# A two-block transformer kernel: the step-size stage opens the first state-space group, and the second norm comes from sums formed in the output stage

## What is computed

```python
def rms(x):      return x * rsqrt(mean(x * x, -1) + 1e-6)
# first block, end
x1 = x + merged @ w_out[layer]
h  = rms(x1) * g_final                     # input of the second block
# second block, mixer
u  = rms(h) * m_norm
zxbcdt = u @ m_in                          # z, conv channels (x, B, C), and dt: 32 columns, one per head
xbc = silu(causal_depthwise_conv(xbc, conv_w, conv_b))
dt  = softplus(dt + dt_bias)
A   = -exp(A_log)
# per chunk of 128 tokens
acum = cumsum(dt * A)                      # decays of the scan come from exp(acum)
...                                        # chunked scan over x, B, C with dt and acum
h = h + gated_and_normed(y) @ m_out
```

## Time and profile before

| | |
|---|---|
| median of 3 runs | 3327.12 us (3324.29 to 3329.75) |
| profiled execution | 3331.93 us, of it the span from first to last instruction 3330.4 us |
| busy: PE, DVE, ACT, POOL | 3112.3 us (93%), 1831.2 (55%), 1394.0 (42%), 682.2 (20%) |
| mean granted TensorE clock, share of full speed | 0.967 |
| output stage, PE's products | 1295.8 to 1385.9 us |
| step-size stage, up to PE's first product of the state-space stage | 1385.9 to 1460.2 us |
| state-space stage | 1460.2 us to about 2270 us |

### The profile page before, as it was taken

How to read it: one execution, slowest core, us unless ns; L and a number is a source line. 1 busy time by engine, 2 the same in 40 slices (tenths; PEclk the granted TensorE clock), 3 DMA queues, 4 the chain that set the end, 5 groups by cost and what they waited for, 6 DMA issues and landing times. The chain is left out here.

```text
span 3330.4 us, 41838 instructions
## 1 busy us (share of the span) xinstructions
PE 3112.3 (93%) x15516; PEld 2601.6 (78%) x15516; DVE 1831.2 (55%) x2485; ACT 1394.0 (42%) x2093; POOL 682.2 (20%) x455
## 2 busy tenths in 40 slices
PE   6999999999999999779999999998899999997799
PEld 5788887888888887657787877776778888886677
DVE  4344222666666533356757666576357777776343
ACT  4333212555555422234334242343246666666331
POOL 3100002222222200211001020010234444443110
PEclk9999999999999999879999999998999999998899
DMA  2111222121111223102111121211111111111321
GB/s 98 41 50 42 70 76 64 58 64 58 51 58 57 93 103 139 33 27 74 48 58 64 45 83 39 70 51 57 69 53 41 43 39 39 39 39 45 120 71 55
DMA packets 55763, 201.69 MB, mean 61 GB/s; under 512 B 6432, under 2 KB 9376, under 8 KB 55328
## 3 DMA queue, kind: packets, MB, share of 16 engines
q1 hardware_dynamic: 46176, 166.76, 15.2%
q0 software_dynamic: 9408, 32.51, 3.1%
HBM read 167.66 MB, written 23.20 MB: 57 GB/s over the span
## 5 line engine op out<-in xcount | busy, mean ns | idle before, releaser
L114 ACT ACTIVATE whi<-wraw 128x1024 fp32r<-128x1024 f32 x208 | 218.4, 1051 | 452.4 <-PE out_D L127 67.6
L119 DVE TENSOR_TENSOR wlo<-wraw,whi 128x1024 fp32r<-128x1024 f32 x173 | 232.8, 1345 | 154.7 <-ACT whi L114 151.1
L125 PE MATMUL ssm_D<-x1hi,whi 128*128 128x512 f32 x640 | 260.2, 407 | 4.4 <-DVEq L1792 4.4
L125 PE MATMUL b_D<-x1hi,whi 128*128 128x512 f32 x640 | 256.0, 400 | 8.5 <-DVEq L1002 6.6
L127 PE MATMUL ssm_D<-x1hi,wlo 128*128 128x512 f32 x640 | 253.3, 396 | 0.0
L126 PE MATMUL ssm_D<-x1lo,whi 128*128 128x512 f32 x640 | 252.8, 395 | 0.0
L126 PE MATMUL b_D<-x1lo,whi 128*128 128x512 f32 x640 | 251.2, 392 | 0.0
L127 PE MATMUL b_D<-x1hi,wlo 128*128 128x512 f32 x640 | 251.0, 392 | 0.0
L2232 DVE TENSOR_TENSOR_SCAN stick_keep<-stick_keep 128x896 f32<-128x896 f32 (+7 forms) x128 | 215.7, 1686 | 43.4 <-ACT stick_keep L2140 42.1
L2371 POOL TENSOR_TENSOR stick_rows<-stick_rows,stick_keep 128x896 f32<-128x896 f32 (+7 forms) x128 | 162.5, 1272 | 272.6 <-DVE stick_keep L2232 272.3
L125 PE MATMUL stick_D<-x1hi,whi 128*128 128x512 f32 x512 | 210.6, 411 | 8.1 <-DVE x1lo L152 8.1
(11 more groups left out here) (413 smaller groups left out, 7982.1 us busy)
## 6 DMA issues: line engine op xcount, KB each, us to landing
wraw<-w_dram SPq DMA_DIRECT2D x208, 512.0 KB, 3.6
sq<-acum_rows SPq DMA_DIRECT2D x32, 512.0 KB, 3.7
att_bias<-alibi_dram SPq DMA_DIRECT2D x16, 512.0 KB, 3.6
stack<-stack POOLq DMA_DIRECT2D x32, 256.0 KB, 3.7
x_sb<-xT_dram SPq DMA_DIRECT2D x8, 512.0 KB, 8.6
branch_a<-sq POOLq DMA_DIRECT2D x8, 512.0 KB, 3.5
y_b<-att_y POOLq DMA_DIRECT2D x8, 512.0 KB, 3.0
f<-y_b SPq DMA_DIRECT2D x2, 2048.0 KB, 8.7
```

Source lines behind the costliest of these rows:

```text
L114: act.activation(self.whi[:, s, :, :], self.wraw[:, s, :, :], ACT.Copy).then_inc(self.w_hi, 1)
L119: dve.tensor_tensor(self.wlo[:, s, :, :], self.wraw[:, s, :, :], self.whi[:, s, :, :].bitcast(F32), ALU.subtract).then_inc(self.w_lo, 1)
L125: pe.matmul(out, self.whi[:, s, w0, :], xhi[:, k, cols], start=start, stop=False)
```

## The change

The output stage gets its own function, `stage_out`, written out without a loop. x is no longer brought into a tensor of its own: SP loads tile k of x into `f_sb` as soon as DVE has split that tile of `merged` (8 transfers of 512 KB, ahead of the stage's weight loads on SP). For tiles 0 to 6 ACT squares x1 and also x1 * g_final, and POOL keeps two sums, in `acc` and in `R`. The stage also loads and splits `w_dt`, now 32 columns wide, and multiplies the gains g_final * m_norm into `decay.gain`. h is not formed here.

`stage_dt` is gone. In `stage_ssm`, which is written out four times instead of looping on all engines, group 0 begins with what is left of it:

- `start()` on ACT and DVE: split x1 * decay.gain into `xhi`/`xlo` (unnormed), square tile 7 twice; POOL adds those squares. Since the norm factors are one number a token, they are put in later: R of the first group's scaling now holds the product of both norms' factors, 1/root1 * 1/root2, with root2 worked out from the second sum and 1/root1.
- On PE: `decay_tile` (the 48 products for dt), the first half of tile 0, `base_sums` (both norm sums), `turn_rows`, the second half, then `spread_factor(rt)`; after tile 1 `spread_factor(K.rtok)`, after tile 2 `decay_sums`; after tile 5 a wait for all of `f_done`, `copied` and `v_step`.
- On DVE behind tile 0 `step_sizes` (the softplus), behind tile 2 `decay_sums`, behind tile 3 `decay_ends`, and behind tiles 2, 3, 4 and 5 two tiles each of `final_norm`, which forms h = x1 * g_final * (1/root1) in `f_sb` from the factor spread in `pY`, and counts `f_done`.
- On ACT behind tile 2 `copy_sums`, behind tile 3 `decay_factors` (three exponentials). SP writes the sums to DRAM between two weight loads of the group.

```diff
@@ stage_out @@
+def stage_out(K, f_sb, xhi, xlo, x_dram, decay):
...
+                for k in range(KT):
+                    sp.wait_ge(x_lo, k + 1)
+                    sp.dma_start(f_sb[:, k, :], x_dram[:, k, :]).then_inc(x_land[k], 16)
+                K.load_ahead(sp, name)
...
+                    for i in range(2):
+                        if n >= 2:
+                            act.wait_ge(acc_done, 2 * n + i - 3)
+                        act.activation(K.sq[:, i, :] if n else accs[i][:, :], f_sb[:, n, :], ACT.Square,
+                                       scale=K.gain("g_final", n) if i else 1.0).then_inc(sq_done, 1)
...
@@ stage_ssm, pe @@
-                    for c in range(6):
+                    if g == 0:
+                        decay_tile()
+                        units(g, 0, 0, KT)
+                        base_sums()
+                        turn_rows()
+                        units(g, 0, KT, 2 * KT)
+                        pe.wait_ge(rt_step, 5)
+                        spread_factor(rt)
+                        units(g, 1, 0, 16)
+                        pe.wait_ge(r_base, 1)
+                        spread_factor(K.rtok)
+                        units(g, 2, 0, 16)
+                        decay_sums()
+                    for c in range(3 if g == 0 else 0, 6):
                         units(g, c, 0, 16)
+                    if g == 0:
+                        pe.wait_ge(copied, 3)
+                        pe.wait_ge(v_step, 13)
+                        pe.wait_ge(f_done, KT)
...
-                with pe.Fori(0, GROUPS) as g:
+                for g in range(GROUPS):
                     group(g)
@@ stage_ssm, act @@
+                def decay_factors():
+                    act.wait_ge(v_step, 12)
+                    act.activation(e_acum[:, :], acum[:, :], ACT.Exp).then_inc(a_step, 1)
+                    act.activation(dte[:, :], dte[:, :], ACT.Exp).then_inc(a_step, 1)
+                    act.activation(e_end[:, :], end[:, :], ACT.Exp).then_inc(a_step, 1)
...
                         act.activation(dst, dst, ACT.Silu).then_inc(cv_s, 1)
+                        if g == 0 and c == 2:
+                            copy_sums()
+                        if g == 0 and c == 3:
+                            decay_factors()
@@ stage_ssm, dve @@
+                def decay_ends():
+                    dve.wait_ge(a_step, 6)
+                    step(dve.tensor_tensor(dte[:, :], dte[:, :], dt[:, :], ALU.mult))
+                    step(dve.tensor_scalar(acum[:, :], acum[:, :], -1.0, None, ALU.mult))
+
+                def final_norm(k0, k1):
+                    dve.wait_ge(spread_base, 2)
+                    for k in range(k0, k1):
+                        dve.scalar_tensor_tensor(f_sb[:, k, :], f_sb[:, k, :], K.gain("g_final", k), pY[:, :],
+                                                 ALU.mult, ALU.mult).then_inc(f_done, 1)
...
                         split(g, c + 2)
+                        if g == 0:
+                            if c == 0:
+                                step_sizes()
+                            elif c == 2:
+                                decay_sums()
+                            elif c == 3:
+                                decay_ends()
+                            if c >= 2:
+                                final_norm(2 * c - 4, 2 * c - 2)
```

More of the change, by code:

```diff
@@ L1262, in _ @@
             @block.tensor
             def _(pe):
[L1264 to L1286, removed]
@@ L1287, in _ @@
-                last.then_inc(t_step, 1)
-                pe.matmul(pA[:, 0:W], tri[:, :], dA[:, :], start=True, stop=True)
-                pe.matmul(pA[:, W:2 * W], K.ones[:, :], dA[:, :], start=True, stop=True).then_inc(t_step, 1)
+                for n in range(KT):
+                    pe.wait_ge(K.w_lo, n + (n0 + 1))
+                    if n >= 2:
+                        pe.wait_ge(added, n - 1)
+                    K.dense(pe, D[:, n % 2, :], n % 2, xhi, xlo, x_lo if n == 0 else None).then_inc(mm, 1)
@@ L1311, in _ @@
[L1311 to L1317 removed]
+                act.activation(decay.hi[:, :, :], raw[:, :, :], ACT.Copy).then_inc(w_done, 1)
@@ new lines, in _ @@
+                dve.wait_ge(w_done, 1)
+                dve.tensor_tensor(decay.lo[:, :, :], raw[:, :, :], decay.hi[:, :, :].bitcast(F32), ALU.subtract)
+                dve.tensor_tensor(decay.gain[:, :], K.vec[:, VEC["g_final"]:VEC["g_final"] + KT],
+                                  K.vec[:, VEC["m_norm"]:VEC["m_norm"] + KT], ALU.mult)
+                for n in range(KT):
+                    dve.wait_ge(mm, n + 1)
+                    dve.wait_ge(x_land[n], 16)
+                    dve.tensor_tensor(f_sb[:, n, :], D[:, n % 2, :], f_sb[:, n, :], ALU.add).then_inc(added, 1)
+                    K.split_lo(dve, n // 2 + (n0 // 2 + 1), n % 2)
@@ L1395, in stage_ssm @@
         xd_odd = scratch[:, GT - 1, :]
+        W = NC * SH
+        with ExitStack() as shared:
+            small = lambda n, shape: shared.enter_context(nc.sbuf_tensor("dt_" + n, shape, F32))
+            rows = small("rows", [SH, S])
+            v, e, l, d, r, dA, end = (small(n, [P, W]) for n in ("v", "e", "l", "d", "r", "dA", "end"))
+            part2, root2, rtok2, rt = (small(n, [P, NC]) for n in ("part2", "root2", "rtok2", "rt"))
         with ExitStack() as shared:
@@ L1640, in _ @@
                 act.sem_inc(cb_copy, 1)
-                with act.Fori(0, GROUPS) as g:
+                start()
+                for g in range(GROUPS):
                     group(g)
@@ L1794, in _ @@
                     dve.sem_inc(q, 1)
-                with dve.Fori(0, GROUPS) as g:
+                start()
+                for g in range(GROUPS):
                     group(g)
```

276 lines of the change are left out of this document (166 added, 110 removed).

## The result

The kernel after takes 3301.27 us (median of 4 runs, 3292.86 to 3305.29), the kernel before on the same chip 3328.43: a ratio of 0.9915, with a 95% interval of 0.990 to 0.993. The profiled execution after took 3305.29 us, its span 3303.8, against 3331.93 and 3330.4 before: 26.6 us less by either. The forecast was 3300.5 for the median and 3305.3 for the profiled run.

The account below looks back on a forecast made before the run. PE bounds the state-space stage; a chain through ACT, DVE and POOL bounds the hole before it. Terms sum to 117.3 us against 142.5; with 1.4 for one wait, gain 26.6: 3327.1 - 26.6 = 3300.5 us, range 3286 to 3314.

Parts of the forecast that it names:

- The hole: Stretch from the output stage's last product to the state-space stage's first, 73.8 us before, bound by an ACT, DVE, POOL chain.
- Item 2: From the last output product to the decay tile's first product PE idles 6.9 us.
- Item 3: Decay tile of 48 products, 14 of them slow: 13.8 us, with DVE's splits staying ahead of PE.
- rival B: Clock stays low at the start, through decay tile, sums and tile 0: gain about 5 us, 3322 us; chance 0.10.
- Item 5: Small products between the convolution tiles (base sums, turn, two spreads, cumulative sums): together 9.3 us.
- Items 6 to 8: PE's waits for DVE ahead of tiles 1, 2 and 5: 2.2, 0.8 and 2.9 us.
- Item 9: PE's wait ahead of the z products until all of h is written: 10.3 us, then 2.9 us for a slow restart.
- +2.9 for the restart and -1.4 for one wait: Z products restart slowly, 2.9 us more; PE's wait for DVE's weighing in the first z tile goes, 1.4 us less.
- A: Written-out loops shorten PE's waits for DVE in all four groups: 15 us more gain, 3286 us; chance 0.14.
- C: The waits keep the clock down through tile 5: 64 us lost, 3362 us; chance 0.06.
- The fail sign: The prediction fails if one of the three later groups changes by more than 3 us.
- Item 10's limit: Slow products follow a wait of 1.98 us but not 1.76; waits ahead of tiles 1 and 5 cost 1.8 each, net 2.8.

Follow-up runs that it names:

- `sums_apart`: The kernel after with the two sets of norm sums parted, the first right behind the decay tile, the second eight units later: 3300.28 us in one run.
- `ends_later`: The kernel after with DVE's two tiles of h in tile 3 ahead of the two steps that need ACT's exponentials: 3295.74 us in one run.
- `r_halves`: The kernel after with DVE's copy of R in two halves, each ahead of the scaling that needs it: 3298.85 us in one run.
- `late_wait`: The kernel after with PE's three waits moved from ahead of the first z product to behind the first 14 z units: 3287.96 us, ratio 0.9882.
- `loops_only`: The kernel before with only the state-space stage's group loops written out on all five engines: 3317.36 us against 3326.12, ratio 0.9971.
- `placed`: The kernel after with moved waits, parted sums, h first and R in halves, plus three small tensors laid where y_sb will be: 3274.36 us, ratio 0.9843.
- `loops_again`: A second look at the kernel before with only the state-space stage's group loops written out: 3318.04 us in one run.
- `apart`: The kernel after with the small products in one piece ahead of the six convolution tiles, no longer between them: 3308.78 us, ratio 0.9939.
- `split_later`: The kernel after with moved waits, parted sums, h first, R in halves, and DVE's first output weight split moved behind the skip: 3283.81 us, ratio 0.9873.

## Why the prediction was right, point by point

**The hole** was sized well: 115.7 us up to the first z product where the sum without the slow restart had 114.4.
- Item 2, first product: 6.5 us, forecast 6.9. Item 3, decay tile: 13.3 against 13.8; DVE's splits stayed ahead, so rival B did not happen.
- Item 5, small products: 4.8 for base sums and turn against 4.5, 2.65 for the cumulative sums against 2.7. Wrong was that nothing follows from them: 12 products behind the base sums were slow and cost 2.4 us. The text had it only as a bound ("a third slow stretch, 1.8 more"). `sums_apart` and the three kernels built on it show that the norm sums in one piece are its cause.
- Items 6 to 8: waits of 2.2, none and 2.6 us, forecast 2.2, 0.8 swallowed, and 2.9 (item 8's own terms add up to 14.0 behind the tile's end, not the 13.8 it states, which would make 3.1). All three stand on DVE's time to spare in a tile, and `ends_later` and `r_halves` show that reading right.
- Item 9: 9.8 us against 10.3, and products slow from 1502.4 to about 1507. `late_wait` puts its worth, with the restart, at 11.8.
- The Trainium skill ("ScalarE: Activation LUTs", What ACT_TABLE_LOAD costs) charges 1.38 us of drain with each table load. The load here began 0.01 us after the Silu's end and took 1.28 us, and the exponential began 0.02 us after that (1473.46 and 1474.76), so the trace does not agree, and the wait ahead of tile 5 came out by the row.

**The rest of the stage** came out right for wrong reasons. The sum gave it +2.9 for the restart and -1.4 for one wait; measured is nothing, 744.9 us from the first z product to the next stage in both. In it are at least four things: the restart; the weighing's waits, 3.5 us less, not because PE stands first (the step named in the sum) but because the loops are written out, as `loops_only` shows without any stand; one slow stretch less, in the fourth group; and 3.6 us more for output products that follow each other more slowly (47.1 to 47.2 us a group instead of the 46.2 of `placed`), which nobody looks for in a diff. The last two were not in the text at all. That the four cancel, and the whole came out at the forecast, is luck.

**The rivals.** A was half right: written-out loops alone bring 8.8 us to the kernel before, and halve the weighing's waits, though not the skip's. The argument against it, that register rows are worked off while the engine is busy, failed: DVE's three taps take 3.92 us in a row now and took 4.14 in loops. The Trainium skill ("Runtime: NRT & Kernel Launch", Instruction fetch mechanics) names a stall at the branch as one price of a loop; the trace shows none on PE, which is busy 10.00 of 10.00 us at the turn both in loops and in `loops_only` (1660 to 1670 us), and shows the price in the waits for DVE. In the kernel after little of it is seen: the new layout takes back 3.6 us, and slow products stand behind three of the four skip's waits. C did not happen; after each of the waits the clock was back within 9 to 12 products.

**The fail sign** that the prediction set, a change of more than 3 us in one of the later groups, did not come: their pitch is 201.1 us on average in both. But this mean hides a gain and a loss.

## What to carry to other kernels

See how much of a gain comes from the shorter chain before working on what hides it: with the small products in one piece, this change kept 21.5 of the 25.0 us between the marks. Where several semaphores are waited for at one place, see which of the next instructions need each; moving one wait behind 14 units of products was worth 11.8 us. After a change of allocation compare the spacing of products in stages that the diff does not touch.

## What the runs showed of the hardware

**The clock falls behind small products too.** Behind 4.8 us of norm sums and turn without a wait the granted clock was 0.5 for the next products; cut to 2.4 us, with 24 large products ahead, it stayed full. Ahead of the convolution tiles a wait of 1.67 us was not followed by slow products, waits of 2.2 and more always were; in the scan 1.97 to 2.00 us ahead of the last turn went both ways, and of the waits for the weighing 1.63, 1.86 and 2.01 were followed by slow products, those of 1.61 and less were not. Item 10's limit between 1.76 and 1.98 was too simple. The Trainium skill ("TensorE: Matmul & The Clock Gate", What's actually happening) says that the gate judges on a schedule of its own which runs on regardless of the program. That would fit one wait with two outcomes; no run here shows the schedule itself, and why `loops_only` and `loops_again` had none in eight groups stays open.

**Where a tensor lies can set the pace of products**: 226.8 to 227.0 ns against 232.4 to 233.2 at the full clock, with the stage's tensors, y among them, 896 bytes further up. Other things that lie there were moved too, so that it is y's own place is likely, not shown.

**DVE and POOL took turns.** While POOL's last two adds of squares ran, DVE's last split took 3.44 us instead of 1.28, and POOL's second add 3.38 instead of 2.40:

```profile
1400.11 2.46 POOL L1935 TENSOR_TENSOR acc<-acc,sq 128x1024 f32<-128x1024 f32 x1 [17.09 <-ACT sq L1584]
1402.53 3.38 POOL L1935 TENSOR_TENSOR R<-R,sq 128x1024 f32<-128x1024 f32 x1
```

```profile
1400.22 3.44 DVE L1712 SCALAR_TENSOR_TENSOR x1lo<-f,decay_gain,x1hi 128x1024 fp32r<-128x1024 f32 x1
```

DVE's split ends at 1403.66, 1.09 us after the first add (1402.57). The Trainium skill ("SBUF — State Buffer", SBUF: two separate sides) says that an op of DVE with two SBUF inputs and one of GpSimd hold a shared pair of ports for the whole instruction, whichever starts first; the rows agree. In `apart`, `sums_apart` and `split_later` it went the other way round: the split took 1.28 us, POOL's first add 3.63 to 3.64 and its second 2.39 to 2.41. It cost nothing here: PE's decay products ran on without a wait.
